# GpSimd computes both halves of the weights' low parts in the second layer's d_out and feed-forward stages

## The chip, the cores and the metric

One core of one Trainium2 chip runs the whole program. The metric is the device time of one execution in microseconds (us), as the median of several runs; less is better.

## The reference, cut to what matters

A two-layer transformer block for 256 tokens of 1024 channels, with 256 context tokens that the first layer updates too. Each layer mixes four branches, multiplies by `w_out`, and then runs a gated feed-forward network:

```python
def _merge(gate_logits, ys, w_out):          # gl, and y_a, y_b, y_c, y_d = branch @ w_x_out
    g = jax.nn.sigmoid(gate_logits).reshape(B, L, N_BRANCH, D_MODEL)
    return jnp.sum(g * jnp.stack(ys, axis=2), axis=2) @ w_out

def _swiglu(h, w_in, w_out):
    gate, up = jnp.split(h @ w_in, 2, axis=-1)
    return (jax.nn.silu(gate) * up) @ w_out

x = x + gt1 * o
x = x + gt2 * _swiglu(_modulate(x, g_ffn[l], sh2, sc2), w_ffn_in[l], w_ffn_out[l])
```

In the second layer (`l == 1`) only the 256 tokens of `x` are carried on, so matrix products there are 256 columns wide (512 in the first layer).

## The kernel before, in words

All weights come as a stream of slabs of 128 x 2048 numbers (1 MB), each the weights of two output tiles of 128 channels (`t` = 0 and 1) for up to eight input tiles `k`. A layer has 104 slabs. Stages use them in the order of `STAGES`: c_in, kv, q, d_in, c_out, b_out, a_cu, a_b, a_out, d_out, w_out, and then ff_in0, ff_out0, ff_in1, ff_out1, ff_in2, ff_out2. The slabs alternate between two buffers `s` = 0 and 1, and a pair of slabs has the number `m`.

Matrix products are made in a split form for accuracy: weights and activations are each a high part (`WH`; `HH`, `ZH`) and a low part (`WL`; `HL`, `ZL`), and `products` issues three matmuls, WH x high, WH x low, WL x high. A slab is thus 8 x 2 x 3 = 48 matmuls (36 in ff_out2, which has six input tiles).

A slab goes through four engines. SyncE's queue loads it into `RAW[s]` once both halves of the low part of the slab before it in that buffer are made (`lo_done[s]`). ScalarE's `high(m, s)` waits for the load and for TensorE's `tile_done[s]` of the slab before it in that buffer, and copies the slab in two halves to `WH`, with `hi_done[s]` counted up at each. Then each half needs its low part, `WL = RAW - WH`, one subtraction of 128 x 1024 numbers:

- in GpSimd's `low(m, s, h)`. GpSimd runs only these. It makes both halves, h = 0 and then h = 1, of every slab that follows a stage in `POOL_WHOLE` (all stages of the first layer, too), and only h = 0 elsewhere;
- in VectorE's `low(m, s)`, which makes h = 1 elsewhere. It stands in VectorE's instruction order behind the work on the tiles of the slab before (`stage` calls `body` and then `low`).

A slab's low part is made while the slab before it in its buffer has been used, so the name in `POOL_WHOLE` decides who makes the slabs one pair later: "d_out" stands for the last three pairs of d_out and the first of w_out.

TensorE's `begin(m, s, halves)` waits for `lo_done[s]` (2 halves, or only the first) and for `slab_out[s]`, which says that the results of the slab two before have been taken out of their banks. Where `halves` is 1, `second_half` waits for the second half after k = 0..3 of the first tile, 12 matmuls later. `in_order` gives 1 where GpSimd makes both halves, and 2 where they come from two engines in no fixed order. The last pair of d_out is written out by hand without `halves`, so it waits for both:

```python
b = pair_base(l, "d_out") + 3
for s in range(2):
    slab(b, s, [(H, W), (Z, W)], mods=..., order=(1, 0) if s else (0, 1))
```

Work of VectorE near the change. In ff_in (`ff_in`): it multiplies three times for the gated unit (`p`, `z` into PSUM bank 7), and makes `ZL` from bank 7 and `ZH` (`z_low`). In d_out (`gated`): it multiplies a gate with a tile in PSUM and adds it to a row of `S`. During the last slab of d_out it makes `ZL` from the first seven rows of `S` (7 calls of `z_low`, from `S` and `ZH`, both in SBUF), then does `gated` for that slab, and, when ScalarE has copied the last row to `ZH`, the eighth `z_low`. w_out's first slab needs row k of `ZL` at its input tile k. Every engine works its instructions off in order.

Of the kernel before, what the change touches and what calls it, by code (L numbers as in the profile page):

```python
# [22 lines left out]
DEPTH = 2  # L23
# [36 lines left out]
def conv_taps(stage, n):  # L60

    first = 0
    for name, shares in CONV_SHARES.items():
        if name == stage:
            first += sum(shares[:n])
            return conv_order()[first:first + shares[n]]
        first += sum(shares)
    raise KeyError(stage)


POOL_WHOLE = ("c_in", "kv", "q", "d_in", "c_out", "b_out", "a_cu", "a_b", "a_out", "w_out")
WARM_UP = {NT: 11, NX: 7}
GELU_C = 0.7978845608028654
GELU_A = 0.044715
# [19 lines left out]
def pair_base(layer, stage):  # L94

    n = layer * LAYER_SLABS
    for name, k in STAGES:
        if name == stage:
            return n // 2
        n += k  # L100
    raise KeyError(stage)
# [21 lines left out]
def build(nc, stream, modw, lruw, xT, cT, prm, rope, consts, outT):  # L123
    with ExitStack() as ctx:
# [74 lines left out]
        def row(t, j, w=NT, a=0):  # L199

            return t[:, j * NT + a:j * NT + a + w] if isinstance(j, int) else t[:, ds(j * NT + a, w)]
# [204 lines left out]
        def _(pool):  # L406
# [11 lines left out]
            for l in range(DEPTH):  # L418
                for name, n in STAGES:
                    first, halves = pair_base(l, name) + 1, 0 if name == "c_in" else 2 if l == 0 or name in POOL_WHOLE else 1  # L420
                    if halves == runs[-1][2]:
# [11 lines left out]
        def _(pe):  # L433
# [10 lines left out]
            def in_order(l, name, first):  # L444

                i = [x for x, _ in STAGES].index(name)
                if first:
                    l, name = (l, STAGES[i - 1][0]) if i else (l - 1, STAGES[-1][0])
                return l <= 0 or name in POOL_WHOLE

# [686 lines left out]
        def _(dve):  # L1137
            V = nc.vector

            def tt(out, x, y, op):  # L1140
                return V.tensor_tensor(out, x, y, op)  # L1141
# [9 lines left out]
            def stage(l, name, body, some=None):  # L1151
# [4 lines left out]
                def one(i, s, more=True):  # L1156
                    dve.wait_ge(tile_done[s], 2 * (i + b) + 2)
                    body(2 * i + s, s, i + b)
                    if l == DEPTH - 1 and more and name not in POOL_WHOLE:
                        low(i + (b + 1), s)  # L1160
# [8 lines left out]
            def low(m, s):  # L1169
                dve.wait_ge(hi_done[s], 2 * m + 2)  # L1170
                x = slice(s * SLAB + HALF, (s + 1) * SLAB)
                tt(WL[:, x], RAW[:, x], WH[:, x].bitcast(F32), SUB).then_inc(lo_done[s], 1)

            def z_low(n, w, src):
                return tt(row(ZL, n, w), src, row(ZH, n, w).bitcast(F32), SUB)
# [37 lines left out]
            for l in range(DEPTH):  # L1213
# [180 lines left out]
                b = pair_base(l, "c_in")  # L1394
# [22 lines left out]
                def gated(which, first=False, at=0):  # L1417
                    def body(n, s, m):
                        sa = a[which + "_a"]
                        dve.wait_ge(sa.sem, sa.at(n, "sg"))  # L1420
                        if first:
                            tt(row(S, n, W), tmp(at + s, 0, W), bank(2 * s + 1, W), MUL).then_inc(slab_out[s], 1)
                        else:
                            sv = a[which + "_v"]
                            dve.wait_ge(slab_out[1 - s], m + (1 + s))
                            tt(bank(7, W), tmp(s, 0, W), bank(2 * s + 1, W), MUL).then_inc(sv.sem, 1)
                            dve.wait_ge(sv.sem, sv.at(n, "t"))
                            tt(row(S, n, W), row(S, n, W), bank(7, W), ADD).then_inc(slab_out[s], 1)
                    return body
# [16 lines left out]
                b = pair_base(l, "kv")  # L1446
                kv = a["kv_v"]
# [60 lines left out]
                b = pair_base(l, "d_in")  # L1508
# [22 lines left out]
                b = pair_base(l, "c_out")  # L1531
                for n in range(KC):
                    s, m = n % 2, b + n // 2
# [9 lines left out]
                b = pair_base(l, "b_out")  # L1543
                for n in range(KC):
                    s, m, taps = n % 2, b + n // 2, conv_taps("b_out", n)
# [13 lines left out]
                b = pair_base(l, "a_cu")  # L1559
                for n in range(KC):  # L1560
                    s, m = n % 2, b + n // 2
# [21 lines left out]
                b = pair_base(l, "a_b")  # L1583
                for n in range(KC // 2):
                    s, m = n % 2, b + n // 2
# [50 lines left out]
                b = pair_base(l, "d_out") + 3  # L1636
                for s in range(2):
                    if s:
                        for k in range(KC - 1):
                            dve.wait_ge(a["ws_a"].sem, k + 1)  # L1640
                            z_low(k, W, row(S, k, W)).then_inc(a["ws_v"].sem, 1)
                    dve.wait_ge(tile_done[s], 2 * b + 2)
                    gated("do")(6 + s, s, b)
                    if l == DEPTH - 1 and s == 0:
                        low(b + 1, s)
                if l == 0:
                    modulation(16, 32, MOD_FIRST + 8, ("m3", None), 1, "g_ffn", 32)
                dve.wait_ge(a["ws_a"].sem, KC)
                z_low(KC - 1, W, row(S, KC - 1, W)).then_inc(a["ws_v"].sem, 1)
                if l == DEPTH - 1:  # L1650
                    low(b + 1, 1)

                def residual(n, s, gt, t):

                    ins = []
                    for c in range(C):
                        x = row(X, 2 * n + t, NX, c * NX)
                        g = MOD[:, ds(2 * n + (t + gt + 48 * c), 1)] if not isinstance(n, int) else \
                            MOD[:, 2 * n + t + gt + 48 * c:2 * n + t + gt + 48 * c + 1]
                        ins.append(stt(x, bank(2 * s + t, NX, c * NX), g, x, MUL, ADD))  # L1660
                    return ins
# [5 lines left out]
                def added_and_summed(name, gt, after, nm):  # L1667
# [4 lines left out]
                    for n in range(KC // 2):  # L1672
# [9 lines left out]
                        residual(n, s, gt, 1)[-1].then_inc(slab_out[s], 1)  # L1682
                        if l == DEPTH - 1 and name not in POOL_WHOLE and n < (2 if last else 3):
                            low(m + 1, s)
# [143 lines left out]
```

## Time and profile before

| what | us |
|---|---|
| median of 3 runs (lowest, highest) | 2185.84 (2185.17, 2187.21) |
| the profiled execution's own time | 2178.32 |
| its span in the trace | 2176.5 |
| TensorE matmul busy | 2073.4 (95%) |
| VectorE busy | 1101.1 (51%) |
| ScalarE busy | 912.9 (42%) |
| GpSimd busy | 825.5 (38%) |

The profile is of one execution. Times in it are us from the start of its span. A matmul's end is modelled, so the pace of TensorE is read from the starts of its matmuls. The releaser that stands behind an instruction is the event that ended the idle time before it.

### The profile page before, as it was taken

The page shows a single profiled execution, that of the slowest core. Times are in us where ns is not written, and L with a number is a line of the kernel's source. Part 1 is how long each engine was busy: PE and PEld are TensorE (multiplying, and loading weights), DVE is VectorE, ACT ScalarE, POOL GpSimd, SP SyncE. Part 2 cuts the span into 40 slices and gives each one's busy share as a digit, 9 for nine tenths or more (in the row PEclk, how much of TensorE's full clock was granted, in tenths as well). Part 3 has the DMA queues.
Part 4 walks back from the last instruction along what each step waited for, and adds up shares of the span by engine and source line. Part 5 has one row for each costly group of instructions (what it writes and reads, how often), then busy time and mean ns, then how long its engine had stood idle before and what let it go on. Part 6 is the DMA issues. An engine that isn't in the chain of part 4 may idle for free.

```text
span 2176.5 us, 31338 instructions
## 1 busy us (share of the span) xinstructions
PE 2073.4 (95%) x11836; PEld 1722.8 (79%) x11836; DVE 1101.1 (51%) x2031; ACT 912.9 (42%) x1439; POOL 825.5 (38%) x348
## 2 busy tenths in 40 slices
PE   6999899999999999999999999999799989999997
PEld 4777677888777777777777778676799989899997
DVE  6894344567789342223111111589545876444445
ACT  5894344222222332323212212489555434544343
POOL 1003222344434333323333434400546877653333
PEclk9999999999999999999999999999999999999999
DMA  8222111222222224554624322322223544344453
GB/s 329 78 78 78 59 59 58 78 97 88 87 96 97 78 78 159 209 212 174 232 95 176 135 97 97 135 78 76 99 103 131 184 164 168 143 174 155 174 174 135
DMA packets 38264, 278.32 MB, mean 128 GB/s; under 512 B 4368, under 2 KB 4368, under 8 KB 4752
## 3 DMA queue, kind: packets, MB, share of 16 engines
q1 hardware_dynamic: 38160, 276.87, 35.0%
q8 instruction: 74, 1.21, 0.2%
q14 instruction: 30, 0.25, 0.0%
HBM read 275.80 MB, written 1.05 MB: 127 GB/s over the span
## 4 chain that ended last, share of the span: by engine, by line
PE 77%; DVE 10%; ACT 8%; issue 3%; DMA 1%; POOL 1%; DVEq 0%; ACTq 0%; SPq 0%; POOLq 0%
PE PS L435 74%; ACT WH L751 2%; DVE PS L1144 2%; PE PS L516 2%; ACT TMP L751 1%; ACT S L751 1%; ACT L751 1%; DVE ZL L1141 1%; ACT CD L751 1%; PE PS L669 1%; DVE SM L1147 1%; DVE TMP L1141 1%; DVE PS L1141 1%; ACT ZH L751 1%; POOL WL L410 1%
## 5 line engine op out<-in xcount | busy, mean ns | idle before, releaser
L410 POOL TENSOR_TENSOR WL<-RAW,WH 128x1024 fp32r<-128x1024 f32 x344 | 825.3, 2418 | 1333.6 <-ACT WH L751 1333.5
L435 PE MATMUL PS<-HH,WH 128*128 128x512 f32 (+1 forms) x2272 | 804.8, 354 | 34.0 <-DVE ZL L1141 12.8
L435 PE MATMUL PS<-HL,WH 128*128 128x512 f32 (+1 forms) x2272 | 781.2, 344 | 0.0
L435 PE MATMUL PS<-HH,WL 128*128 128x512 f32 (+1 forms) x2272 | 781.2, 344 | 0.0
L751 ACT ACTIVATE WH<-RAW 128x1024 fp32r<-128x1024 f32 x416 | 417.4, 1052 | 680.3 <-PE PS L435 659.3
L435 PEld LDWEIGHTS PS<-HH,WH 128*128 128x128 f32 x2272 | 431.2, 190 | 108.7 <-issue 40.4
L435 PEld LDWEIGHTS PS<-HL,WH 128*128 128x128 f32 x2272 | 431.4, 190 | 58.3 <-issue 6.0
L435 PEld LDWEIGHTS PS<-HH,WL 128*128 128x128 f32 x2272 | 430.7, 190 | 55.7
L435 PE MATMUL PS<-ZH,WH 128*128 128x512 f32 (+1 forms) x992 | 340.3, 343 | 18.0 <-DVE ZL L1141 15.8
L435 PE MATMUL PS<-ZL,WH 128*128 128x512 f32 (+1 forms) x992 | 337.4, 340 | 0.0
L435 PE MATMUL PS<-ZH,WL 128*128 128x512 f32 (+1 forms) x992 | 337.2, 340 | 0.0
L1144 DVE SCALAR_TENSOR_TENSOR PS<-G,PRM,PS 128x512 f32<-128x512 f32 (+1 forms) x464 | 254.2, 614 | 0.3
L435 PEld LDWEIGHTS PS<-ZH,WH 128*128 128x128 f32 x992 | 187.9, 189 | 47.5 <-DVE ZL L1141 19.2
L435 PEld LDWEIGHTS PS<-ZH,WL 128*128 128x128 f32 x992 | 188.1, 190 | 23.0
L435 PEld LDWEIGHTS PS<-ZL,WH 128*128 128x128 f32 x992 | 188.0, 190 | 22.1
L751 ACT ACTIVATE TMP<-PS 128x256 f32<-128x256 f32 (+1 forms) x230 | 105.1, 462 | 212.1 <-PE PS L516 97.0
L1141 DVE TENSOR_TENSOR TMP<-TMP,PS 128x512 f32<-128x512 f32 (+1 forms) x56 | 31.6, 564 | 303.0 <-ACT TMP L751 288.3
L1141 DVE TENSOR_TENSOR PS<-TMP,PS 128x256 f32<-128x256 f32 (+1 forms) x84 | 46.2, 550 | 203.7 <-ACT TMP L751 177.6
L1144 DVE SCALAR_TENSOR_TENSOR X<-PS,MOD,X 128x256 f32<-128x256 f32 (+1 forms) x96 | 41.8, 478 | 146.9 <-PE PS L435 146.9
L1141 DVE TENSOR_TENSOR WL<-RAW,WH 128x1024 fp32r<-128x1024 f32 x72 | 100.7, 1417 | 10.5 <-ACT WH L751 10.4
L751 ACT ACTIVATE ZH<-PS 128x256 f32 (+1 forms) x60 | 27.3, 461 | 96.4 <-DVE PS L1141 63.0
L1144 DVE SCALAR_TENSOR_TENSOR G<-G,PS 128x512 f32 (+1 forms) x16 | 8.9, 556 | 111.8 <-ACT G L751 111.8
(159 smaller groups left out, 1636.9 us busy)
## 6 DMA issues: line engine op xcount, KB each, us to landing
RAW<-in_stream SPq DMA_DIRECT2D x208, 1024.0 KB, 4.8
CD<-in_modw SPq DMA_DIRECT2D x42, 1024.0 KB, 7.1
CD<-in_lruw SPq DMA_DIRECT2D x2, 2048.0 KB, 8.5
X<-in_xT SPq DMA_DIRECT2D x2, 1024.0 KB, 7.2
S<-in_modw SPq DMA_DIRECT2D x2, 1024.0 KB, 13.0
G<-in_modw SPq DMA_DIRECT2D x2, 1024.0 KB, 20.8
RAW<-in_modw SPq DMA_DIRECT2D x1, 1024.0 KB, 16.0
TMP<-in_modw SPq DMA_DIRECT2D x1, 1024.0 KB, 17.8
```

What stands on the lines that cost most here:

```text
L410: nc.gpsimd.tensor_tensor(WL[:, a:b], RAW[:, a:b], WH[:, a:b].bitcast(F32), ALU.subtract)\
L435: return nc.tensor.matmul(out, lhs, rhs, start=start, stop=stop)
L516: last = nc.tensor.matmul(PS[32 * g:32 * g + 32, 5 + slot, 0:2 * P], SILC[:, 32 * k:32 * k + 32], w[:, k * 2 * P:(k + 1) * 2 * P], start=k ...
L669: last = nc.tensor.transpose(bank(4 + u, P, q * P), PR[u % 2][:, q * P:(q + 1) * P], IDENT)
L751: return nc.scalar.activation(out, in_, f, **kw)
L1141: return V.tensor_tensor(out, x, y, op)
L1144: return V.scalar_tensor_tensor(out, x, sc, y, op0, op1)
L1147: return V.tensor_scalar(out, x, s1, s2, op0, op1) if op1 is not None else V.tensor_scalar(out, x, s1, None, op0)
```

## The change

GpSimd makes both halves for the slabs that follow d_out, ff_in0, ff_out0, ff_in1, ff_out1 and ff_in2 in the second layer. VectorE's part of them is gone. `in_order` gives `halves` = 1 for these slabs where TensorE's stages ask it. Only the slabs that follow ff_out2 (its own last pair) stay split.

```diff
-POOL_WHOLE = ("c_in", "kv", "q", "d_in", "c_out", "b_out", "a_cu", "a_b", "a_out", "w_out")
+POOL_WHOLE = ("c_in", "kv", "q", "d_in", "c_out", "b_out", "a_cu", "a_b", "a_out", "w_out",
+              "d_out", "ff_in0", "ff_out0", "ff_in1", "ff_out1", "ff_in2")
...
                     dve.wait_ge(tile_done[s], 2 * b + 2)
                     gated("do")(6 + s, s, b)
-                    if l == DEPTH - 1 and s == 0:
-                        low(b + 1, s)
                 if l == 0:
                     modulation(16, 32, MOD_FIRST + 8, ("m3", None), 1, "g_ffn", 32)
                 dve.wait_ge(a["ws_a"].sem, KC)
                 z_low(KC - 1, W, row(S, KC - 1, W)).then_inc(a["ws_v"].sem, 1)
-                if l == DEPTH - 1:
-                    low(b + 1, 1)
```

## Rows read from the trace of the kernel before

**Rows 1.** The page, busy time of each engine (share of the span) and instructions.
```profile
PE 2073.4 (95%) x11836; PEld 1722.8 (79%) x11836; DVE 1101.1 (51%) x2031; ACT 912.9 (42%) x1439; POOL 825.5 (38%) x348
```

**Rows 2.** Instructions on tile WL by VectorE from 1850 on: min/median/max ns, first and last start.
```profile
L1141 DVE TENSOR_TENSOR WL<-RAW,WH x40: 1210/1216/2591, 1897.7 to 2157.8; 128x1024 fp32r<-128x1024 f32 x40
```

**Rows 3.** Timeline of TensorE, feed-forward of the second layer: start, us, instruction, idle before.
```profile
1978.32 0.28 PE L435 MATMUL PS<-HH,WL 128*128 128x256 f32 x1
1978.67 0.38 PE L435 MATMUL PS<-HH,WH 128*128 128x256 f32 x1
...
2018.06 0.38 PE L435 MATMUL PS<-ZH,WH 128*128 128x256 f32 x1 [1.68 <-DVE ZL L1141]
...
2049.37 0.28 PE L435 MATMUL PS<-HH,WL 128*128 128x256 f32 x1
2049.95 0.39 PE L435 MATMUL PS<-HH,WH 128*128 128x256 f32 x1 [0.30 <-DVE WL L1141]
...
2132.43 0.28 PE L435 MATMUL PS<-HH,WL 128*128 128x256 f32 x1
2132.78 0.38 PE L435 MATMUL PS<-HH,WH 128*128 128x256 f32 x1
```

**Rows 4.** Chain of work that ended last, one slab of ff_in0: start, us, what.
```profile
2000.71 1.23 DVE WL L1141
...
2002.06 11.55 PE PS L435 x96
```

**Rows 5.** Timeline of GpSimd and VectorE for the same slab.
```profile
1997.56 2.40 POOL L410 TENSOR_TENSOR WL<-RAW,WH 128x1024 fp32r<-128x1024 f32 x1 [3.66 <-ACT WH L751]
...
2000.37 0.42 DVE L1141 TENSOR_TENSOR ZL<-PS,ZH 128x256 f32 x1 [0.67 <-ACT ZH L751]
```

**Rows 6.** Timeline of GpSimd, b_out of the second layer.
```profile
1716.27 4.77 POOL L410 TENSOR_TENSOR WL<-RAW,WH 128x1024 fp32r<-128x1024 f32 x2 [0.77 <-ACT WH L751]
...
1727.53 4.76 POOL L410 TENSOR_TENSOR WL<-RAW,WH 128x1024 fp32r<-128x1024 f32 x2 [0.78 <-ACT WH L751]
```

**Rows 7.** Loads of RAW, issue to landing, 1970 to the end.
```profile
DMA to landing us min/median/max: 4.7/4.8/5.9
```

**Rows 8.** Timeline of GpSimd and TensorE, last pair of d_out.
```profile
1918.46 2.40 POOL L410 TENSOR_TENSOR WL<-RAW,WH 128x1024 fp32r<-128x1024 f32 x1 [3.32 <-ACT WH L751]
1922.66 0.28 PE L435 MATMUL PS<-HH,WH 128*128 128x256 f32 x1
```

**Rows 9.** Timeline of all engines, from d_out to w_out.
```profile
1929.63 2.41 POOL L410 TENSOR_TENSOR WL<-RAW,WH 128x1024 fp32r<-128x1024 f32 x1 [3.22 <-ACT WH L751]
1931.66 1.46 DVE L1141 TENSOR_TENSOR WL<-RAW,WH 128x1024 fp32r<-128x1024 f32 x1
1933.04 2.43 DVE L1141 TENSOR_TENSOR ZL<-S,ZH 128x256 fp32r<-128x256 f32 x7
1935.53 2.36 POOL L410 TENSOR_TENSOR WL<-RAW,WH 128x1024 fp32r<-128x1024 f32 x1 [3.49 <-ACT WH L751]
1936.74 1.43 DVE L1141 TENSOR_TENSOR ZL<-S,ZH 128x256 fp32r<-128x256 f32 x1 [0.48 <-ACT ZH L751]
...
1938.23 0.39 PE L435 MATMUL PS<-ZH,WH 128*128 128x256 f32 x1 [1.68 <-DVE ZL L1141]
```

**Rows 10.** Timeline of GpSimd and VectorE, from c_out to b_out.
```profile
1702.93 2.69 POOL L410 TENSOR_TENSOR WL<-RAW,WH 128x1024 fp32r<-128x1024 f32 x1 [1.18 <-ACT WH L751]
1703.30 2.62 DVE L1141 TENSOR_TENSOR ZL<-CD,ZH 128x256 fp32r<-128x256 f32 x1
1705.59 2.54 POOL L410 TENSOR_TENSOR WL<-RAW,WH 128x1024 fp32r<-128x1024 f32 x1
1705.84 2.57 DVE L1141 TENSOR_TENSOR ZL<-CD,ZH 128x256 fp32r<-128x256 f32 x1
```

**Rows 11.** Windows: stretch, TensorE busy (matmuls), granted clock, DMA share, GB/s.
```profile
1892.00:1895.00 3.00, 3.00 (x16) 0.50 0.73 303
...
1967.00:1970.40 3.40, 3.40 (x18) 0.54 0.75 275
```

## The prediction, made before the change was run

> **What bounds the kernel now.** I read the page first. TensorE is busy 95% of the span, VectorE 51% and GpSimd 38% [rows 1]: time can only come from, or go to, the idle of TensorE, some 100 us in all. So I looked at TensorE alone, from d_out of the second layer to the end, where the change acts. In the timeline one matmul starts every 0.1173 us at full speed, so a slab of 48 lasts 5.63 us, and any greater step between two starts is a wait. After each wait the next matmul is 0.11 longer (0.39 for 0.28 us), which goes with the wait.
>
> The steps in the feed-forward fall into two kinds. At the first slab of a pair in ff_in there is a small one: 0.35 us between starts at 1978.67, 0.58 at 2049.95, 0.35 at 2132.78 [rows 3]. There are eleven: four in ff_in0's stretch, four in ff_in1's, three in ff_in2's, of 0.31 to 0.57 us each with the 0.11. The chain of waits says what ends them: VectorE's low part of the weights, 2000.71 to 2001.94, directly before TensorE's 2002.06 [rows 4]. VectorE does it last, after the z_low of 2000.37 [rows 5], though its input was there long before. The second kind is one large wait in each ff_out, such as 1.68 us at 2018.06, for the last z_low of ff_in [rows 3]. No low part of a weight is in that chain.
>
> ff_out and d_out have no small steps. d_out ends in a wait of 1.68 us for a z_low at 1938.23 [rows 9].
>
> **What is removed.** VectorE loses 38 of its 40 subtractions from 1897.7 on [rows 2]: 8 behind d_out, 8, 4, 8, 4 and 6 behind the feed-forward stages, at some 1.2 us or, where they wait, up to 2.6 us. VectorE is not the bound, so this is worth only what TensorE waited for. Of the eleven small steps the last of each ff_in stage (at the start of ff_out) saves nothing: TensorE would come to the large wait so much earlier, and what ends that does not move. Eight are left, from 0.33 to 0.57 us (steps less the usual 0.12, plus 0.11), together 3.06 us. **Term A: -3.1 us.** Next in line is slab_out behind the z_low: it ends at 2000.79 [rows 5], and TensorE would want the slab at 2001.77, so 0.9 us are left.
>
> **What is added.** GpSimd makes two halves of 2.40 one after the other. That this keeps up is seen in b_out of the second layer, which is made so already: pairs of halves of 4.77 us, two slabs in 11.26 us, with 0.8 us idle between [rows 6], TensorE without a wait. In ff_in the first half begins at 1997.56 [rows 5], so the second ends at 2002.3. TensorE starts the slab at 2001.77 and asks for the second half 12 matmuls later, at 2003.2. Cover 0.9 us: nothing. Were the cover gone, each microsecond too late would cost one on each of 30 slabs.
>
> The loads begin when both halves are made, at 2002.4 here. The usual 4.8 us [rows 7] bring them to 2007.2, and ScalarE wants the slab at 2007.65. The longest of 5.9 us would come 0.65 late, which the 0.9 above takes up. Nothing.
>
> **The last pair of d_out** is written out without `halves`, so TensorE waits for both. Its first slab: GpSimd starts at 1918.46, and TensorE takes the slab up at 1922.66 with no wait [rows 8]. With two halves it is ready at 1918.46 + 4.77 + 0.1 = 1923.3: a wait of 0.66, and 0.11 behind it. The second slab follows 5.6 later and is ready at 1928.9 against a wanted 1929.0. **Term B: +0.8 us.** It could be 0 to 1.6 if the second slab just misses.
>
> **From d_out to w_out.** Here is the dear part. z_low from S and ZH has both inputs in SBUF, and such an instruction does not run beside GpSimd's subtraction. At 1936.74 a z_low lasts 1.43 in place of 0.41 us: it begins its 0.3 us when GpSimd's half ends at 1937.89 [rows 9]. From c_out to b_out, where GpSimd makes two halves in a row, it is worse: a z_low of 1703.30 lasts 2.62 us, GpSimd's second half starts at 1705.59, and the z_low of 1705.84 lasts 2.57 us [rows 10]. So between two halves exactly one z_low gets through, and the next waits a whole half. The Trainium skill says so too (SBUF — State Buffer, "Who interferes with whom"): a VectorE instruction with two SBUF inputs contends with a GpSimd instruction that reads SBUF, and the lock is held for the whole instruction. The trace agrees, with 2.57 us against 0.42 for one that reads PSUM [rows 5, 10]; by the rule and by the rows the sum is the same, but without the lock it would be the rival "nothing caught" below.
>
> Worked through on the times of before, for the eight z_low of d_out's last slab [rows 9]:
> - GpSimd 1929.63 to 1932.04, first half. VectorE comes to its first z_low at 1931.66, where it had the subtraction. It is done at 1932.3.
> - GpSimd's second half, new: 1932.0 to 1934.55. The second z_low waits for it: done 1934.8.
> - The third, fourth and fifth at 0.34 each (2.43 us for seven): 1935.8.
> - GpSimd has the next slab from 1935.53. By the rows above its first half ends near 1938.2, and the sixth z_low at 1938.5.
> - GpSimd's second half, new: to 1940.7. The seventh z_low: 1941.0.
> - Before, the seventh ended at 1935.47. The gate's multiply and sum, ScalarE's copy and an unhindered last z_low ended 1.7 us later, at 1937.15 (then held up until 1938.17 by the lock). Now: 1942.7.
>
> TensorE goes on at 1942.8 in place of 1938.23. **Term C: +4.5 us.** If the sixth z_low slips in before GpSimd takes the lock at 1935.53, the seventh ends at 1938.5. The last is then asked for at 1939.8, waits for the second half until 1940.7 and ends at 1941.0: +2.8. I take 4.5, since the sixth would be 0.2 us after GpSimd's start. The bounds are 0 and 4.5.
>
> **The clock.** In those 7 us TensorE has some nine matmuls between three waits. Twice nearby, TensorE's granted clock fell to its lower level of 1.2 GHz after such gaps: 16 matmuls in 3.0 us at 0.50 [rows 11], after two waits for z_low with three matmuls between them, and again at 0.54 after the gap between w_out and ff_in0. Each time some 16 matmuls came 0.213 us apart in place of 0.117, which is 1.5 us. It did not fall after the single waits of 1.7 us. **Term D: +1.5 us**, bounds 0 and 3.0 (two such stretches).
>
> **The sum.** -3.1 + 0.8 + 4.5 + 1.5 = +3.7 us on a span of 2176.5, or on the profiled execution's own 2178.3. The runs' median is 2185.84, 7.5 above the profiled one. The waits should be the same in both, so I add the difference: 2189.5 us, or +0.17%. A measurement of this kernel tells about 0.2% (4.4 us) from no change, so this counts as no difference, on the slow side.
>
> **Rivals.**
> - *The clock stays low for two stretches* at the start of w_out (the other side: slower). For it speaks that here three waits come in 7 us, against two in 4 us before the fall of 1892. Against it: both falls seen lasted one stretch. The price is 1.5 more, sum +5.2, 2191.0 us. It decides from some 23 matmuls at the low clock on, with term C at its full 4.5.
> - *Nothing caught.* The z_low calls slip between GpSimd's halves, or TensorE takes w_out later anyhow. A and B alone: -2.3 us, 2183.5. For it: the phases are known only to 0.2 us. Against: between c_out and b_out the two engines took turns in just this order [rows 10].
> - *The all-GpSimd rhythm doesn't hold* in the feed-forward: loads land 0.65 late on 15 pairs, +10 us, 2199. For it: 5.9 us was seen once [rows 7]. Against: b_out holds it, with the same loads [rows 6].
> - *More is gained than A.* The large waits of ff_out would have to shrink as well; the chain gives no reason.
>
> The Trainium skill also speaks against the whole idea (GPSIMD Engine Reference, "Key points"): for elementwise work VectorE is about twice as fast. The trace agrees, 2.40 against 1.22 us. By that rule, each moved half paid in full, 38 x 1.18 = 45 us would be lost; but the halves lie beside TensorE's slabs of 5.63 us.
>
> **How the numbers follow.** Forecast with terms C and D between their bounds, +0.6 to +4.3 us: 0.48. Clock low for two stretches or as much again elsewhere: 0.25. Nothing caught: 0.15. Rhythm: 0.06. More gained: 0.06. Faster by over 0.2% is only the last, and a little scatter of the runs: 0.07. Slower by over 0.2% is the clock, the rhythm, and the upper edge of the forecast: 0.33. Within: 0.60. The range goes from "nothing caught", 2183.5, to the clock's 2191.0 with the runs' scatter of some 1.5 us, 2192.5.
>
> **What would show it in the profile after.** No small steps in ff_in, and GpSimd's halves in pairs of 4.77, would show A. A wait for GpSimd of 0.7 us near the seventh slab of d_out would show B. For C: z_low from S at 2.5 us twice or three times, and TensorE's wait at w_out's start grown from 1.7 to some 6 us in pieces. For D: a window of 3 us at 0.5 behind it. Wrong would be: the step at 1938 not later than before, or waits for DMA or GpSimd in ff_in.

## The result and the profile after

The changed kernel takes 2187.36 us (median of 12 runs, 2184.42 to 2192.69), the kernel before 2183.26 (12 runs, 2178.08 to 2187.21). The ratio is 1.0021, 95% interval 1.0011 to 1.0031: by it some 4.6 us slower, from 2.4 to 6.8 (the two medians lie 4.1 us apart). The prediction had said +3.7 us or +0.17%, counted that as no difference, and gave "slower by over 0.2%" 0.33. The measured ratio lies on that line.

The page after, the lines of busy time and of GpSimd's group:

```profile
PE 2076.8 (95%) x11836; PEld 1727.2 (79%) x11836; DVE 1049.7 (48%) x1993; ACT 913.2 (42%) x1439; POOL 917.9 (42%) x386
...
L411 POOL TENSOR_TENSOR WL<-RAW,WH 128x1024 fp32r<-128x1024 f32 x382 | 917.7, 2424 | 1249.2 <-ACT WH L752 1249.2
```

VectorE has the 38 instructions less, and 51 us less work; GpSimd has 38 more, and 92 us more [rows 1]. Neither shows in the time by itself. TensorE's timeline after does, at the places where it waits:

```profile
1924.32 0.39 PE L436 MATMUL PS<-HH,WH 128*128 128x256 f32 x1 [0.44 <-POOL WL L411]
...
1936.74 0.39 PE L436 MATMUL PS<-ZH,WH 128*128 128x256 f32 x1 [0.41 <-DVE ZL L1142]
...
1940.26 0.39 PE L436 MATMUL PS<-ZH,WH 128*128 128x256 f32 x1 [1.82 <-DVE ZL L1142]
...
1942.75 0.38 PE L436 MATMUL PS<-ZH,WH 128*128 128x256 f32 x1 [1.87 <-DVE ZL L1142]
...
1944.45 0.58 PE L436 MATMUL PS<-ZH,WH 128*128 128x256 f32 x1 [0.89 <-DVE ZL L1142]
...
2024.81 0.50 PE L436 MATMUL PS<-ZH,WH 128*128 128x256 f32 x1 [2.00 <-DVE ZL L1142]
```

There is a new wait for GpSimd before d_out's seventh slab. At w_out's start stand four waits for z_low, 5.0 us, where one of 1.68 stood [rows 9]. The wait at ff_out0's start has grown from 1.68 to 2.00 [rows 3]: TensorE comes there 0.3 us earlier, and what it waits for does not come earlier.

Why w_out waits four times is seen in the timeline of GpSimd and VectorE after, from d_out to w_out:

```profile
1931.46 2.40 POOL L411 TENSOR_TENSOR WL<-RAW,WH 128x1024 fp32r<-128x1024 f32 x1 [1.66 <-ACT WH L752]
...
1933.62 0.53 DVE L1142 TENSOR_TENSOR ZL<-S,ZH 128x256 fp32r<-128x256 f32 x1
1933.82 2.59 POOL L411 TENSOR_TENSOR WL<-RAW,WH 128x1024 fp32r<-128x1024 f32 x1
1934.07 2.62 DVE L1142 TENSOR_TENSOR ZL<-S,ZH 128x256 fp32r<-128x256 f32 x1
...
1937.43 2.49 POOL L411 TENSOR_TENSOR WL<-RAW,WH 128x1024 fp32r<-128x1024 f32 x1 [1.02 <-ACT WH L752]
1937.62 2.58 DVE L1142 TENSOR_TENSOR ZL<-S,ZH 128x256 fp32r<-128x256 f32 x1
1939.89 2.52 POOL L411 TENSOR_TENSOR WL<-RAW,WH 128x1024 fp32r<-128x1024 f32 x1
1940.13 2.57 DVE L1142 TENSOR_TENSOR ZL<-S,ZH 128x256 fp32r<-128x256 f32 x1
...
1943.97 0.43 DVE L1142 TENSOR_TENSOR ZL<-S,ZH 128x256 fp32r<-128x256 f32 x1 [0.48 <-ACT ZH L752]
```

The second, sixth and seventh z_low (1934.07, 1937.62, 1940.13) each enter while a half of GpSimd runs, and end some 0.28 us behind its end. Between two halves in a row one z_low gets through, no more. This is the sequence that the prediction worked out, shifted by 1.7 to 1.9 us (1.05 came before d_out, 0.71 with the wait there).

The clock in two windows after (stretch, TensorE busy and matmuls, granted clock, DMA share, GB/s):

```profile
1944.80:1949.70 4.90, 4.90 (x24) 0.50 0.38 159
...
2025.10:2028.30 3.20, 3.20 (x16) 0.50 0.27 54
```

Behind w_out's waits 24 matmuls run at the lower level of 1.2 GHz, behind ff_out0's wait 16. The stretch at 0.54 that the kernel before had at ff_in0's start [rows 11] is not in this profile.

In ff_in the small steps are gone, and GpSimd keeps the rhythm of b_out [rows 6]. Timeline of GpSimd after, ff_in0:

```profile
1998.99 4.77 POOL L411 TENSOR_TENSOR WL<-RAW,WH 128x1024 fp32r<-128x1024 f32 x2 [0.78 <-ACT WH L752]
2004.72 4.76 POOL L411 TENSOR_TENSOR WL<-RAW,WH 128x1024 fp32r<-128x1024 f32 x2 [0.95 <-ACT WH L752]
```

The two profiled executions differ by 8.0 us of span (2184.5 and 2176.5), more than the medians do. From landmark to landmark on TensorE the lag of the one after grows so: 1.05 us before d_out (nothing changed there); +5.17 to the last z_low wait at w_out (1938.23 to 1944.45, less the 1.05); +2.42 to ff_in0's first matmul (1965.23 to 1973.87); -1.89 to ff_out0's wait; +0.85 to ff_out1's; -0.86 to ff_out2's; +1.26 to the end.

Set side by side matmul by matmul, the two timelines say more. At the eight small steps of ff_in the lag shrinks from 8.01 to 6.75 us in ff_in0 (starts 1972.75 and 1980.76, to 2007.80 and 2014.55), from 8.57 to 7.55 in ff_in1 and from 7.60 to 6.74 in ff_in2: 3.14 us in all. Another 0.63 goes in ff_in0's first slab, where the kernel before had its stretch at the lower clock. The last step of each ff_in stage takes off 0.2 us more, and the longer wait behind it gives that back. Against this stand 1.5 us of low clock behind ff_out0's start and 1.1 us of waiting for a late load before the last slab. And from 2029.6 to 2092.3 a slab of 48 matmuls takes 5.70 us in place of 5.63, at the same granted clock of 1.00: 0.7 us, 0.4 of it inside ff_in1's figure, that nothing in the change explains.

### The profile page after: what moved, and what is told of

It reads as the page before. It is cut to its first block, busy times and chain, and to the rows that moved or that the text cites. A ratio compares the mean times of both kernels' runs of the same rounds, so it can differ in the third digit from the quotient of the medians.

```text
span 2184.5 us, 31352 instructions
## 1 busy us (share of the span) xinstructions
PE 2076.8 (95%) x11836; PEld 1727.2 (79%) x11836; DVE 1049.7 (48%) x1993; ACT 913.2 (42%) x1439; POOL 917.9 (42%) x386
## 3 DMA queue, kind: packets, MB, share of 16 engines
HBM read 275.80 MB, written 1.05 MB: 127 GB/s over the span
## 4 chain that ended last, share of the span: by engine, by line
PE 78%; DVE 9%; ACT 8%; issue 3%; DMA 1%; POOL 1%; DVEq 0%; ACTq 0%; SPq 0%; POOLq 0%
PE PS L436 75%; DVE PS L1145 2%; PE PS L517 2%; ACT WH L752 2%; DVE ZL L1142 1%; ACT S L752 1%; ACT TMP L752 1%; ACT L752 1%; ACT CD L752 1%; POOL WL L411 1%; PE PS L670 1%; DVE SM L1148 1%; DVE TMP L1142 1%; ACT ZH L752 1%; DVE PS L1142 1%
## 5 line engine op out<-in xcount | busy, mean ns | idle before, releaser
L411 POOL TENSOR_TENSOR WL<-RAW,WH 128x1024 fp32r<-128x1024 f32 x382 | 917.7, 2424 | 1249.2 <-ACT WH L752 1249.2
```

The lines of the kernel that those rows point to most:

```text
L411: nc.gpsimd.tensor_tensor(WL[:, a:b], RAW[:, a:b], WH[:, a:b].bitcast(F32), ALU.subtract)\
```

## The experiments

All ran in five rounds against the kernel before. Diffs are against the changed kernel unless said otherwise; `...` marks what is left out of them. Each has one profile. A ratio is of a whole kernel to the kernel before, so 0.0005 is 1.1 us.

**Feed-forward alone** (against the kernel before):

```diff
-POOL_WHOLE = (..., "w_out")
+POOL_WHOLE = (..., "w_out", "ff_in0", "ff_out0", "ff_in1", "ff_out1", "ff_in2")
```

> Only the slabs behind the feed-forward stages go to GpSimd whole; d_out keeps the split, so w_out's start is as before. Theory (the loss lies between d_out and w_out, the gain in ff_in): the eight small steps in ff_in vanish, -3.1 us, and the late load before the last slab of ff_out2 costs +1.2 us: -1.9 us in all, ratio 0.9991, and the wait at w_out's start stays near 1.8 us. Rival (the all-GpSimd rhythm in the feed-forward is what costs): slower than before by 2 to 4 us, with waits of TensorE on GpSimd or loads in ff_in and ff_out.

Measured: 2182.44 us, ratio 0.9992 (0.9983 to 1.0001). Its only wait at w_out's start is 1.69 us, as before. The gain is of the expected size (0.9991 was expected), with an interval that just takes in nothing. It isn't slower, which decides against the rival.

**d_out alone** (against the kernel before):

```diff
-POOL_WHOLE = (..., "w_out")
+POOL_WHOLE = (..., "w_out", "d_out")
...
-                    if l == DEPTH - 1 and s == 0:
-                        low(b + 1, s)
...
-                if l == DEPTH - 1:
-                    low(b + 1, 1)
```

> Only the slabs behind d_out go to GpSimd whole. Theory: +0.7 us at the last pair of d_out, +4.5 us from z_low calls caught between GpSimd's halves, +2.4 us for a stretch at the low clock at the start of w_out: +7 to +8 us, ratio 1.0034, and the waits inside w_out's first slab sum to 6 us. Rival (rhythm in the feed-forward): within 1 us of before.

Measured: 2189.90 us, ratio 1.0025 (1.0014 to 1.0035), the whole loss and a little more, though 2 us less than the 1.0034 expected. Who waited for whom on TensorE, 1936 to 1946:

```profile
PE PS L436 <- DVE ZL L1142: 5.2, 4, 1.9
```

The four waits are there (total, times, longest), and 25 matmuls at the lower clock behind them. The loss is thus in d_out's part, which decides against the rival.

**w_out's first pair split again.** GpSimd makes all of d_out's last three pairs, but for w_out's first pair VectorE's `low` is back at its two places, and TensorE starts this pair when both halves are there.

```diff
+SPLIT_LAST = ((1, "d_out"),)
...
+                    end = pair_base(l, name) + 1 + n // 2
+                    split = (l, name) in SPLIT_LAST
...
+                    runs.append((first, end - split, halves))
+                    if split:
+                        runs.append((end - 1, end, 1))
...
-                return l <= 0 or name in POOL_WHOLE
+                return l <= 0 or name in POOL_WHOLE and not (first and (l, name) in SPLIT_LAST)
...
+                    if l == DEPTH - 1 and s == 0:
+                        low(b + 1, s)
...
+                if l == DEPTH - 1:
+                    low(b + 1, 1)
```

> As the changed kernel, but the second halves of w_out's first pair are VectorE's again. Theory: z_low finds GpSimd with one half at a time, the waits at w_out's start fall back to 1.8 us and the clock doesn't fall there; left are +0.7 in d_out, -3.1 in ff_in, +1.2 in ff_out2: -1.2 us against before, some 5 to 7 us less than the changed kernel. Rival (the cost at w_out comes from the later start of its first slab, or from loads): the waits stay near 6 us.

Measured: 2181.28 us, ratio 0.9987 (0.9978 to 0.9996). Two of the 38 moved instructions taken back turn 4.6 us slower into 2.8 us faster (1.2 faster was expected). VectorE's instructions on ZL there (min, median, max ns), and TensorE's one wait at w_out's start, with no matmul at the lower clock behind it:

```profile
L1147 DVE TENSOR_TENSOR ZL<-S,ZH x8: 412/414/1444, 1940.9 to 1944.8; 128x256 fp32r<-128x256 f32 x8
```

```profile
1946.25 0.38 PE L441 MATMUL PS<-ZH,WH 128*128 128x256 f32 x1 [1.66 <-DVE ZL L1147]
```

**GpSimd held back.** The last run gives VectorE work back, so the lock alone is not yet shown. Here GpSimd still makes everything, but waits for the z_low calls:

```diff
+                    if hi == held:                      # held = pair_base(1, "w_out")
+                        for s in range(2):
+                            for h in range(2):
+                                if s or h:
+                                    pool.wait_ge(L[DEPTH - 1]["ws_v"].sem, KC if s else KC - 1)
+                                low(held, s, h)
```

> As the changed kernel, but at w_out's first pair GpSimd waits: its second half of the first slab until seven z_low are done, the second slab until all eight are. GpSimd still makes all halves. Theory (z_low and GpSimd's subtraction exclude each other): the z_low calls now take 0.34 us each, none 2.5, TensorE waits once, some 1.5 us, for the second half instead, and the time is 5 to 7 us less than the changed kernel's, ratio to before 0.999. Rival (the z_low calls are late for another reason, such as ScalarE's copies): they stay late and the time stays above before.

Measured: 2181.15 us, ratio 0.9987 (0.9977 to 0.9997). First VectorE's instructions on ZL, then TensorE's timeline:

```profile
L1150 DVE TENSOR_TENSOR ZL<-S,ZH x8: 410/412/564, 1939.8 to 1944.7; 128x256 fp32r<-128x256 f32 x8
```

```profile
1944.95 0.35 PE L444 MATMUL PS<-ZH,WH 128*128 128x256 f32 x1 [1.45 <-POOL WL L411]
```

The longest z_low falls from 2619 ns to 564, and TensorE waits once in w_out's first slab, for the second half. (It waits for GpSimd once more, 0.55 us at 1962.83, in a later slab of w_out.) Nothing but the time of GpSimd's two slabs was moved, so z_low was late because GpSimd's subtraction ran.

**Extra matmuls in w_out's waits:**

```diff
+                def keep_warm(k):
+                    for _ in range(14 if l and k > 4 else 0):
+                        mm(bank(5, 2 * P), WH[:, 0:P], row(ZH, 0, 2 * P), True, True)
+                    pe.wait_ge(a["ws_v"].sem, k + 1)
+
-                stage_and_sums(l, "w_out", KC, lambda k: pe.wait_ge(a["ws_v"].sem, k + 1), l, "n2", W, W)
+                stage_and_sums(l, "w_out", KC, keep_warm, l, "n2", W, W)
```

> As the changed kernel, with 14 extra matmuls (their result is not used) before each of the last three waits for z_low in w_out's first slab. Theory: the waits are idle time of TensorE, and filling them with work keeps its clock at the upper level: the 24 slow matmuls vanish, -2.4 us against the changed kernel, the end of the waits stays where it is. Rival (the slow matmuls there have another cause, such as the transfers): they stay, and the time is the changed kernel's.

Measured: 2185.18 us, ratio 1.0010 (1.0001 to 1.0019), 0.0011 or 2.4 us less than the changed kernel, as expected, though the intervals overlap. The windows at w_out's start:

```profile
1938.00:1941.00 3.00, 2.79 (x23) 1.00 0.52 221
1941.00:1946.00 5.00, 4.75 (x41) 1.00 0.62 215
```

The z_low calls still take up to 2624 ns, but the clock stays at its upper level here. In the same profile it fell behind the starts of ff_out1 and ff_out2, where no extra matmuls stood. So, as far as one profile can show it, the idle time is what lets it fall.

**d_out's last pair starts on its first half:**

```diff
-                         order=(1, 0) if s else (0, 1))
+                         order=(1, 0) if s else (0, 1), halves=1)
```

> As the changed kernel, but TensorE starts the slabs of d_out's last pair when the first half of their low part is there. Theory: the wait of 0.6 us for GpSimd before the seventh slab of d_out vanishes and nothing else moves: 0.7 us less than the changed kernel, ratio 1.0018. Rival (the saved time is spent in the longer wait for z_low behind it): the wait vanishes and the time does not change.

Measured: 2187.66 us, ratio 1.0022 (1.0013 to 1.0031). The wait before d_out's seventh slab is gone from the trace, the time has not moved. The waits behind it did not swallow the gain either: from the first of w_out's waits to the last it is 7.7 us in both profiles, and from a matmul of the slab before to the first of them 18.7 us against 19.4. (The waits themselves sum to 4.6 us against 5.0, because some of the matmuls between them ran slower.) So the profile keeps some 0.6 us that the medians do not show. A term of 0.7 us is below what five rounds tell here.

**The mended kernel** joins the last-pair start, SPLIT_LAST for d_out, and SPLIT_LAST for ff_in2:

```diff
+SPLIT_LAST = ((1, "d_out"), (1, "ff_in2"))
...
-                         order=(1, 0) if s else (0, 1))
+                         order=(1, 0) if s else (0, 1), halves=1)
...
```

> As the changed kernel, with VectorE making the second halves again for w_out's first pair and for ff_out2's first pair, and TensorE starting d_out's last pair on its first half. Theory: no wait near d_out's seventh slab, 1.8 us at w_out's start, no late load in ff_out2, no small steps in ff_in: 3 us less than before, ratio 0.9987. Rival (the gain of ff_in is given back by longer waits and clock stretches at the starts of ff_out): ratio 0.9995 or more.

Measured: 2179.57 us, ratio 0.9984 (0.9973 to 0.9994), 3.5 us less than before where 3 were expected. The clock still fell once in its profile, behind ff_out0's start.

**The feed-forward less ff_in2** (against the kernel before):

```diff
-POOL_WHOLE = (..., "w_out")
+POOL_WHOLE = (..., "w_out", "ff_in0", "ff_out0", "ff_in1", "ff_out1")
```

> As the run with the feed-forward alone, but the slabs behind ff_in2 stay split. Theory: two of the eight small steps stay (+0.7 us), and the load of the last slab of ff_out2 comes in time again (-1.2 us): 2.3 us less than before, ratio 0.9989. Rival (the late load is due to the ten slabs of 5.63 us before it running faster, not to who makes the low parts): the wait of 1.1 us in ff_out2 is still there.

Measured: 2182.48 us, ratio 0.9998 (0.9989 to 1.0007): a miss, 2 us too slow for the expectation. The profile shows one cause. Windows behind the starts of ff_out0, ff_out1 and ff_out2:

```profile
2020.70:2024.00 3.30, 3.30 (x17) 0.50 0.40 119
2092.50:2095.80 3.30, 3.30 (x18) 0.51 0.52 164
2153.90:2157.20 3.30, 3.30 (x17) 0.50 0.68 221
```

The clock fell at all three. Each such stretch has 16 matmuls at 0.213 us from start to start in place of 0.117: 1.5 us. In the profile before it fell at none of the three. Over the ten profiles without extra matmuls there (before, after, and the eight runs told above) it fell at 12 of 30 such starts.

**Extra matmuls at these starts.** In four kernels, the kernel before, the mended one, the feed-forward alone, and the feed-forward less ff_in2, 14 matmuls with an unused result stand before the last wait for z_low, in w_out's first slab and each ff_out's of the second layer:

```diff
+                def warm(n):
+                    for _ in range(n if l else 0):
+                        mm(bank(5, 2 * P), WH[:, 0:P], row(ZH, 0, 2 * P), True, True)
...
+                def w_out_row(k):
+                    warm(14 if k == KC - 1 else 0)
+                    pe.wait_ge(a["ws_v"].sem, k + 1)
...
+                    if k == n - 1 and f not in warmed:
+                        warm(14)
+                        warmed.add(f)
```

> The kernel before with the same extra matmuls, nothing else. It measures what the clock stretches at these four starts cost the kernel before: by the theory 0 to 2 us less than before, since its waits there are 0.3 us shorter than the changed kernel's; by the rival nothing.

> The kernel of the mended run with 14 extra matmuls (result not used) before the last wait for z_low in w_out's first slab and in each ff_out's. Theory (each such wait is a chance for the clock to fall for 16 matmuls, 1.5 us): no low-clock stretch behind these starts, 1 to 4 us less than the mended kernel. Rival (the stretches come from elsewhere): the same time as the mended kernel, and stretches still there.

> The feed-forward alone made whole by GpSimd, with the 14 extra matmuls before the last wait for z_low at w_out and at each ff_out. Theory: the low-clock stretches behind ff_out's starts took back part of the gain of ff_in; without them the gain shows: 2.5 to 4 us less than before, ratio 0.9985, and the wait of 1.1 us for the late load in ff_out2 is seen. Rival: the gain of ff_in is smaller than the steps it removes; ratio 0.9992 as without the extra matmuls.

> The same with the slabs behind ff_in2 split as before, and the extra matmuls. Theory: no late load in ff_out2, two small steps left in ff_in2, no low-clock stretches: 3 to 4 us less than before, ratio 0.9983. Rival: the load is late here too, which would put it down to the pace and not to the moment when both halves are made.

| kernel | without extra matmuls | with them |
|---|---|---|
| before | 1 | 0.9996 (0.9987 to 1.0005) |
| mended | 0.9984 (0.9973 to 0.9994) | 0.9980 (0.9970 to 0.9989) |
| feed-forward alone | 0.9992 (0.9983 to 1.0001) | 0.9982 (0.9973 to 0.9991) |
| feed-forward less ff_in2 | 0.9998 (0.9989 to 1.0007) | 0.9973 (0.9962 to 0.9983) |

The mended kernel gains 0.9 us by them, just under the 1 to 4 expected, and within the intervals it could be nothing. With the feed-forward alone (0.9985 expected) the wait for the late load that was expected did not come: the load landed in 4.8 us. The last one (0.9983 expected) came out 2 us faster than expected.

In the four profiles with them the clock fell at none of the 12 starts. The same three places in the last kernel:

```profile
2019.00:2025.00 6.00, 5.64 (x48) 1.00 0.70 209
2090.00:2096.00 6.00, 5.26 (x44) 1.00 0.50 190
2150.00:2156.00 6.00, 5.26 (x45) 1.00 0.60 210
```

It has the lowest median of all: 2177.24 us, 0.9973 (0.9962 to 0.9983), from 8 runs, with 38 - 8 - 6 = 24 of the moved halves at GpSimd. With the extra matmuls its interval overlaps those of the mended kernel and of the feed-forward alone, and without them leaving out ff_in2 looked worse, not better (0.9998 against 0.9992), so which of the three is best is not shown. Only its difference to the same kernel without extra matmuls, 0.0025 or 5.5 us, is clear of both intervals; three stretches at the lower clock, were all three there in every run, would account for 4.6 of it. The kernel before gains nothing that can be told.

## Why the prediction was right, point by point

**The sum.** By the lags of the one pair of profiles, its four terms came to -3.1 + 0.7 + 4.5 + 2.4 = +4.5 us, against +3.7 forecast and 4.1 (medians) or 4.6 (ratio) measured. That the total fits so well is in part luck. The profiled execution of the changed kernel was 8.0 us longer than that of the kernel before, not 4.5: it also came 1.05 us late to d_out and had a fall of the clock in ff_out0, a late load and slower slabs, and none of these is in the sum. How much of them stands in the medians is not known. And the 2189.5 us were built on 2185.84 for the kernel before, from three runs, where twelve give 2183.26; so the forecast came out 2.1 us above the 2187.36 measured.

**Term A, ff_in's small steps, -3.1 us: right.** The steps are gone in the profile after, and the lag shrinks by 3.14 us over them. In the measured times it is less sure. With the feed-forward alone the time falls by 1.7 us (from 3.7 to nothing), and by 3.9 (2.0 to 5.9) when the clock is kept up; the kernel before falls by 0.9 with the same extra matmuls, which leaves 3.0. The cover held too: TensorE waits for no half in ff_in after. The prediction's "ff_out and d_out have no small steps" was a misreading, without consequence: ff_out2 has one of 0.77 us between starts at 2156.21, for VectorE's low part of its own last pair, which stays split, and it is still there after (2162.95).

**Term B, +0.8 us: right.** The new wait in the trace is 0.60 us by its step and 0.11 behind it, 0.71. In the measured time it could not be told.

**Term C, +4.5 us: right, and it is the cause of the loss.** The lag grew by 5.17 us there, 4.46 without B. The order of the calls was as worked out, with the sixth z_low caught, where a slip had been possible. That GpSimd's subtraction is what holds z_low is shown by holding GpSimd back; that it costs this kernel its gain, by "d_out alone" (1.0025) and by the two kernels with the pair mended (both 0.9987). What the Trainium skill says (SBUF — State Buffer, "Who interferes with whom"), that two SBUF inputs on VectorE contend with a GpSimd instruction that reads SBUF, and that the one behind waits for the whole instruction, agrees with the 2.57 to 2.62 us of z_low after.

**Term D, +1.5 us: right in kind, too small.** 24 matmuls came at the lower clock, 16 had been set; the stretch between w_out's last wait and ff_in0 grew by 2.42 us. The extra matmuls there gave back 2.4 us of the changed kernel's time. By the prediction's own sign ("from some 23 matmuls at the low clock on, with term C at its full 4.5") this is its rival of two stretches, which had a chance of 0.25: 24 matmuls, and C at 4.46. The measured loss of 4.6 us lies between the forecast's upper edge, +4.3, and the rival's +5.2. So the mechanism was right, and its size lay between the two.

**What the sum left out** is the clock at ff_out's starts. The prediction held the last step of each ff_in stage to be worth nothing, as the wait behind it takes it up. That is so, but it lengthens this wait, from 1.68 to 2.0 us, and such a wait is where the clock can fall. It fell behind ff_out0's in the profile after and not in that before. In the kernels with the feed-forward untouched it fell at 1 of 6 starts (before, d_out alone), in the other eight at 11 of 24. Sorted by the length of the wait in the same ten profiles, with the single waits at w_out's start counted in, the picture is sharper: behind the 10 single waits of 1.45 to 1.70 us (four at ff_out, six at w_out) it fell never, behind the 26 of 1.97 to 2.70 us, all at ff_out, 12 times. Were the length without meaning, the ten would all be spared by chance in some 1 case of 130. So the step that was "worth nothing" in the prediction most likely has a price: it makes a wait of 1.7 us one of 2.0, and these were followed by 1.5 us of slow matmuls nearly every second time. No run changed the length of a wait alone, and six of the ten short ones stand at another place, so this is argued, not shown.

**"Nothing caught"** is out. **"The rhythm doesn't hold"** is out as a steady cost in ff_in and ff_out, by the pairs of 4.77 us. Single late loads break it: with extra matmuls in w_out's waits a load of 6.6 us was followed by a wait for GpSimd of 0.59 us in ff_in2 (2115.64), and in the mended kernel with extra matmuls one of 6.2 by a wait of 0.16. In the changed kernel one late load showed, before the last slab of ff_out2, as a wait of 1.1 us in the profile after and in that of the feed-forward alone. I took it for a fixed cost of the change, and wrote it so into several expectations. It is not. Issue to landing of that load, in the changed kernel and in the one with GpSimd held back:

```profile
DMA to landing us min/median/max: 6.5/6.5/6.5
```

```profile
DMA to landing us min/median/max: 4.9/4.9/4.9
```

The load is issued 1.2 us before ScalarE takes up the slab before it in both. Before, it was 1.5 us. Where it lands in 4.9 nothing waits; where it takes 6.5 it is late. So the change took 0.3 us of the cover, and the rest is the load's own length in that execution, whose cause is open.

The ratios of the parts add up within their intervals: 0.9992 and 1.0025 make 1.0017, against 1.0021.

## What to carry to other kernels

Before work is moved to GpSimd, look for the VectorE instructions with both inputs in SBUF that stand on the critical path, and at what GpSimd will run just then: here two of 38 moved instructions cost more than all the others gained. Two halves in a row are worse than one, since only one VectorE instruction gets through between them. And where TensorE waits 2 us in a stage change, a few matmuls into a free bank are worth a trial, for the clock may otherwise run the next 16 at half speed; of four kernels here, one was clearly faster for it.

## What was not expected of the hardware

After a single wait of some 2 us on a busy TensorE the clock fell in some profiles and not in others: the wait of 2.0 us at ff_out0's start was followed by 16 matmuls at 0.50 in the changed kernel, and the wait of 2.0 at ff_out1's (2096.92 in its timeline) by none. One load of 1 MB took 6.5 us with nearly the same issue as one of 4.9. And at a granted clock of 1.00 a slab of 48 matmuls takes 5.63 us in some stretches of tens of us and 5.70 in others, in the unchanged kernel with extra matmuls too (5.70 around 2080); the cause is open.
